# Expert passes cut in quarters of 32 rows, experts ordered on the chip by remainder, five weight buffers in both layers

## The chip, the cores and the metric

One Trainium2 chip, of which one core runs the kernel. The metric is the device time of one execution in microseconds (us). Three runs of the kernel before gave 2852.11, 2854.56 and 2857.07 us; their median is 2854.56 us.

## What is computed

A block of two layers over 512 latent tokens and 256 context tokens of 1024 numbers each, all in 32-bit floats. Each layer mixes the tokens (four groups of attention heads) and then sends each token through a mixture of experts. Only that second half is touched here:

```python
idx, wts = _route(h, w_r, b_r)          # sigmoid scores; 8 of 64 experts per token, from 4 of 8 groups
for each expert e:
    y = (silu(x @ wg[e]) * (x @ wu[e])) @ wd[e]      # x: the tokens that chose e; 1024 -> 256 -> 1024
    acc[tokens] += y * weight
f = acc + _swiglu(h, shared expert)
```

Layer 0 routes all 768 tokens (6144 choices of an expert), layer 1 only the 512 latent ones (4096 choices). How many tokens an expert gets is data. With the reference's own inputs the router gives experts 9 to 253 tokens. What matters below is the number of 32-row quarters that a count fills, modulo 4 ("the remainder"); experts 0 to 4 are kept apart, as the change treats them apart:

| | remainder 1 | remainder 2 | remainder 3 | remainder 0 | experts 0 to 4 |
|---|---|---|---|---|---|
| layer 0 | 11 experts | 9 | 21 | 18 | 102, 84, 77, 103, 130 tokens |
| layer 1 | 11 experts | 29 | 16 | 3 | 35, 57, 117, 36, 117 tokens |

Rounded up to halves of 64 rows, the counts fill 127 halves in layer 0 and 93 in layer 1.

## The kernel before

`build` runs, for each layer, the attention stages, then `route`, `experts` and `ffn_residual`. Each is a block in which every engine has its own program; semaphores order them.

`route` (lines 1206 to 1384) picks the experts on DVE, counts the tokens of each (PE, a product with ones), and turns the counts into a table in SBUF that the engines then read with register loads: for each pass the expert of its upper and of its lower 64 rows (`T_E0`, `T_E1`), a word that says which weight buffers it uses (`T_PASS`), the number of passes (`T_COUNT`), and for each expert the number of passes that must be over before its buffer may be loaded (`T_FREE`). An expert takes as many halves of 64 rows as it needs, at least one; the halves stand one behind another in the order of the experts, and two make a pass. DVE does this in a chain of small dependent operations (lines 1341 to 1382); PE helps with small products (1264 to 1281) and has the products of the shared expert (line 257) to do beside it.

`experts` (from 1387) runs a loop over passes, two to a turn, so that their number is rounded up to an even one. One pass i on the engines:

- PE: turns the gathered rows of pass i+1 (line 1555), forms the down products of pass i (1584), turns the hidden units (1562), makes the token list of pass i+3 (1550), and forms the gate and up products of pass i+1 (1575). Every matmul is made once for the upper and once for the lower 64 columns of the tile, `ps[h * HB:(h + 1) * HB, ...]` from buffer `w[h]`, also where both belong to one expert. Which buffers are meant is found by a tree of branches (`by_buffers`) over 2 x NB written-out variants, with NB the number of weight buffers.
- ACT and DVE: silu, the product with the up half, copies out of PSUM, the token list (`mark_slots`, `make_index`), the weight column, and the scaled result Y.
- POOL: one scatter of Y, which adds into `acc_dram` (line 1504), and one gather of the rows X of pass i+3 (1494). A scatter starts when the one before it has landed.
- SP: loads the weights, in the order of the experts, gate and up of expert e (2 MB) and down of e-1 (1 MB), each behind a wait until PE has done the last pass of the expert that held the buffer (`load_gate_up` 1448, `load_down` 1453).

There are five buffers in layer 0 and six in layer 1 (`BUFFERS = (5, 6)`). Buffers 3 and 4 are in use by the shared expert until the experts' stage has begun, so that their first experts come late.

Of the kernel before, what the change touches and what calls it, by code (L numbers as in the profile page):

```python
# [20 lines left out]
F16 = mybir.dt.float16  # L21
I32 = mybir.dt.int32
U32 = mybir.dt.uint32
ALU = mybir.AluOpType
# [3 lines left out]
P = 128  # L28
D = 1024
# [18 lines left out]
U = 2  # L48
STRETCH = 6
HB = P // 2  # L50
T_E0, T_E1, T_PASS, T_COUNT, T_FREE, T_TURNS, TAB_W = (
    1, TABN + 1, 2 * TABN, 4 * TABN, 4 * TABN + 1, 4 * TABN + 1 + E, 4 * TABN + 2 + E)
VAR = 256
AHEAD = 3
BUFFERS = (5, 6)
SHARED, TURNED, EARLY = 3, 4, 0
NTHR = NROW // HB
# [14 lines left out]
C_ID, C_COS, C_SIN, C_COSR, C_SINR, C_PREV, C_NEXT, C_BAND, C_P2, C_NEGP, C_NONE, C_NEGB, C_THR, C_ADD, C_SEL, C_W = (  # L72
    0, 128, 384, 640, 768, 896, 1024, 1152, 1216, 1218, 1219, 1220, 1348, 1360, 1361, 1363)

H_TRI, H_ONE, H_IOTA, H_TIN, H_TST, H_TSTHB, H_TOK, H_W = 0, 128, 256, 384, 448, 512, 576, 588
# [1130 lines left out]
def route(v, l, nt, gm, table, ex, shared):  # L1206
# [10 lines left out]
    s_sel, s_cnt, s_nb, s_slot, s_tab, s_tt = S("chosen"), S("counted"), S("blocks_counted"), S("slots"), S("table_columns"), S("table_turned")  # L1217
    counts = []
    with ExitStack() as scope:
# [9 lines left out]
        cc = sb("cc", [E, NTHR + 2])  # L1229
        nbb = sb("nbb", [E, P], F16)  # L1230
        o1 = sb("o1", [P, E])
        tb = sb("tb", [P, 12])
        fr = sb("fr", [1, E + 2])

        with nc.Block() as block:
# [20 lines left out]
            def _(pe):  # L1256
# [10 lines left out]

                s_nb.wait(pe, 1)
                pe.matmul(ps[:, 6, 0:E], nbb[:, :], csth[0:E, H_TIN:H_TIN + E], start=True, stop=True)
                for i in range(nt):  # L1270
                    out = ps[:, 7, i * E:(i + 1) * E]
                    pe.matmul(out, nbb[:, :], csth[0:E, H_TSTHB:H_TSTHB + E], start=True, stop=False)
# [3 lines left out]
                last.then_inc(s_slot.sem, 1)  # L1276
                shared.gate_up_products(pe, 2, 0)
                shared.gate_up_products(pe, 2, 1)
                s_tab.wait(pe, 1)
                for c in range(3):  # L1280
                    last = pe.matmul(ps[0:1, 6, c * P:(c + 1) * P], tb[:, c:c + 1], v.ident, start=True, stop=True)
# [9 lines left out]
            def _(dve):  # L1291
# [49 lines left out]
                step(dve.tensor_copy(cc[:, NTHR + 1:NTHR + 2], ps[0:E, 6, E:E + 1]))  # L1341
                step(dve.tensor_scalar(cc[:, 0:NTHR], v.cst[0:E, C_THR:C_THR + NTHR], cc[:, NTHR + 1:NTHR + 2], None, ALU.is_lt))
                step(dve.tensor_reduce(cc[:, NTHR:NTHR + 1], cc[:, 0:NTHR], AX, ALU.add))
                dve.tensor_scalar(nbb[:, :], csth[0:E, H_ONE:H_ONE + P], cc[:, NTHR:NTHR + 1], None, ALU.mult).then_inc(s_nb.sem, 1)
# [12 lines left out]
                for h in range(2):  # L1357
                    step(dve.tensor_scalar(o1[:, :], ps[:, 6, 0:E], v.cst[:, C_P2 + h:C_P2 + h + 1], None, ALU.is_le))
                    step(dve.tensor_reduce(tb[:, h:h + 1], o1[:, :], AX, ALU.add))
                step(dve.tensor_scalar(tb[:, 0:2], tb[:, 0:2], float(E - 1), None, ALU.min))  # L1360
                whole(tb[:, 5:6], tb[:, 0:1], 1.0 / NB, -0.5 + 0.5 / NB)
                step(dve.tensor_scalar(tb[:, 7:8], tb[:, 5:6], -float(NB), tb[:, 0:1], ALU.mult, ALU.add))
                step(dve.tensor_tensor(tb[:, 8:9], tb[:, 1:2], tb[:, 0:1], ALU.subtract))
                step(dve.tensor_scalar(tb[:, 2:3], tb[:, 7:8], 2.0, tb[:, 8:9], ALU.mult, ALU.add))
                step(dve.tensor_copy(tb[:, 9:10], ps[:, 6, E - 1:E]))
                whole(tb[:, 10:11], tb[:, 9:10], 0.5, 0.25)
                whole(tb[:, 11:12], tb[:, 9:10], 0.25, 0.375)
                step(dve.tensor_scalar(tb[:, 11:12], tb[:, 11:12], 16.0, None, ALU.mult))
                whole(fr[0:1, 0:E], ps[0:1, 6, 0:E], 0.5, 0.25)
                step(dve.memset(table[0:1, T_PASS:T_PASS + 2 * TABN], 0))  # L1370
                step(dve.memset(table[0:1, T_FREE:T_FREE + NB], 0))
                step(dve.tensor_copy(table[0:1, T_FREE + NB:T_FREE + E], fr[0:1, 0:E - NB]))
                step(dve.tensor_scalar(tb[:, 3:4], tb[:, 5:6], 16.0, 16.0, ALU.mult, ALU.add))
                dve.tensor_scalar(tb[:, 2:3], tb[:, 2:3], float(VAR), tb[:, 3:4], ALU.mult, ALU.add).then_inc(s_tab.sem, 1)
                shared.hidden_units(dve, 1)
                s_tt.wait(dve, 1)
                step(dve.tensor_copy(table[0:1, 0:2 * P], ps[0:1, 6, 0:2 * P]))
                by_pass = table[0:1, T_PASS:T_PASS + 2 * TABN].rearrange("a (p w) -> a w p", w=2)
                step(dve.tensor_copy(by_pass[:, 0, 1:TABN], ps[0:1, 6, 2 * P:3 * P - 1]))
                step(dve.tensor_copy(by_pass[:, 1, 0:TABN - 1], ps[0:1, 6, 2 * P + 1:3 * P]))  # L1380
                step(dve.tensor_copy(table[0:1, T_COUNT:T_COUNT + 1], tb[0:1, 10:11]))
                step(dve.tensor_copy(table[0:1, T_TURNS:T_TURNS + 1], tb[0:1, 11:12]))
    for s, k in ((s_step, counts[0]), (s_ex, 1), (s_wt, 1), (s_ws, 16), (s_clear, 3), (s_sel, 1), (s_cnt, 1), (s_nb, 1), (s_slot, 1), (s_tab, 1), (s_tt, 1)):
        s.stage_over(k)


def experts(v, l, nt, gm, table, ex, shared):
# [4 lines left out]
    pairs = ((nt * P * 8 + E * HB) // HB + 1) // 2  # L1392
# [16 lines left out]
    with ExitStack() as scope:  # L1409
# [9 lines left out]
        cur = sb("cur", [P, nt, 2])  # L1419
# [25 lines left out]
        with nc.Block() as block:  # L1445
            @block.sync
            def _(sp):
                def load_gate_up(w, e, free):
                    sp.wait_ge(gate_up, free + CREDIT)
                    sp.dma_start(wgu[w][:, :, :].rearrange("p k n -> p (k n)"),  # L1450
                                 v.t["exp_gu"][l][bass.ds(e, 1)].rearrange("a p n -> (a p) n")).then_inc(w_gu[w], 16)

                def load_down(w, e, free):
                    sp.wait_ge(down, free + CREDIT)
                    sp.dma_start(wd[w][:, :, :].rearrange("p k n -> p (k n)"),
                                 v.t["exp_d"][l][bass.ds(e, 1)].rearrange("a p n -> (a p) n")).then_inc(w_d[w], 16)
# [10 lines left out]
                sp.wait_ge(gate_up, free_after(NB) + CREDIT)  # L1467
                sp.dma_start(wgu[0][:, :, :].rearrange("p k n -> p (k n)"), v.t["exp_gu"][l, NB]).then_inc(w_gu[0], 16)
# [6 lines left out]
                for e in range(NB + 1 + rounds * NB, E):  # L1475
                    sp.wait_ge(gate_up, free_after(e) + CREDIT)
                    sp.dma_start(wgu[e % NB][:, :, :].rearrange("p k n -> p (k n)"), v.t["exp_gu"][l, e]).then_inc(w_gu[e % NB], 16)
# [519 lines left out]
```

## Time and profile before

| | |
|---|---|
| median of the runs | 2854.56 us |
| the profiled execution: its own time | 2857.52 us |
| its span in the trace | 2855.7 us |
| mean granted clock of TensorE | 0.961 |
| PE busy | 2586.1 us, 91% of the span |
| DVE, ACT, POOL busy | 38%, 20%, 14% |
| HBM read, written | 578.84 MB, 77.99 MB |

The layers stand one behind the other. The expert stage of layer 0 takes about 759 to 1554 us of the span, that of layer 1 about 2179 to 2825 us; `route` stands ahead of each. In the profile "L1575" is line 1575 of the kernel, "PEld" is TensorE's loading of the stationary operand, a 32-bit matmul appears as two records, and "issue" is idle time for which the profile shows no releaser.

### The profile page before, as it was taken

Reading aid. Unit: us, or ns where it says so; the run is one execution under the profiler, and the core shown is the slowest. Engines: PE = TensorE matmul, PEld = TensorE weight load, DVE = VectorE, ACT = ScalarE, POOL = GpSimd, SP = SyncE. Lnnn points to the kernel's source line nnn. Section 1 sums busy time; section 2 is a strip of 40 time slices with the busy share of each in tenths; the row PEclk is TensorE's granted clock in tenths of the full one; section 3 lists DMA queues with packets and bytes.
Section 4 is the critical chain, followed back from the end, with each engine's and each line's share of the span. In section 5 each row is a group of like instructions: output and inputs, shape, how many; then the busy total and the mean of one; then the engine's idle time right before and its main releaser. Section 6 shows DMA issues by size and latency. Waiting matters only on the chain. (4 is left out here: it accounts for less than half of the span.)

```text
span 2855.7 us, 44970 instructions
## 1 busy us (share of the span) xinstructions
PE 2586.1 (91%) x13801; PEld 1281.4 (45%) x13802; DVE 1084.5 (38%) x3199; ACT 585.4 (20%) x1378; POOL 386.9 (14%) x314
## 2 busy tenths in 40 slices
PE   6999989999899999999996588989997999899995
PEld 3566555645433333333332366666553333333331
DVE  3443351534333333333332743451543233233323
ACT  2222341411111111111111341331310111111111
POOL 0000001000022222222221200001000212112122
PEclk9999999999999999999998799999998999999998
DMA  7120203043688998999993402202346999998983
GB/s 273 58 93 30 113 21 143 4 181 128 228 281 310 344 327 281 325 325 323 335 371 98 172 1 93 89 16 116 115 178 251 351 394 398 396 392 306 382 319 112
DMA packets 104984, 619.35 MB, mean 217 GB/s; under 512 B 22832, under 2 KB 23088, under 8 KB 64688
## 3 DMA queue, kind: packets, MB, share of 16 engines
q1 hardware_dynamic: 69744, 525.06, 46.7%
q0 software_dynamic: 33696, 87.63, 12.7%
q10 hardware_dynamic: 1440, 5.24, 0.5%
q8 instruction: 69, 1.13, 0.2%
q14 instruction: 35, 0.29, 0.0%
HBM read 578.84 MB, written 77.99 MB: 230 GB/s over the span
## 5 line engine op out<-in xcount | busy, mean ns | idle before, releaser
L1575 PE MATMUL ps<-wgu,xT 128*64 128x512 f32 x2048 | 454.9, 597 | 3.1 <-issue 3.1
L1575 PE MATMUL ps<-wgu,SGx 128*64 128x512 f32 x1536 | 351.7, 610 | 22.5 <-DMA wgu<-in_exp_gu 18.3
L1504 POOL DMA_INDIRECT ffn_rows<-Y,six x114 | 182.5, 1601 | 1120.0 <-issue 651.1
L678 PE MATMUL ps<-w_in,wgu 128*128 128x512 f32 (+3 forms) x768 | 267.8, 509 | 15.0 <-PEq L435 3.8
L1575 PEld LDWEIGHTS ps<-wgu,xT 128*64 128x64 f32 x2048 | 141.8, 137 | 261.9 <-issue 260.7
L1584 PE MATMUL ps<-wd,hiddenT 128*64 128x512 f32 x1040 | 239.2, 602 | 5.6 <-issue 5.6
L1575 PEld LDWEIGHTS ps<-wgu,SGx 128*64 128x64 f32 x1536 | 110.6, 140 | 223.4 <-issue 217.0
L678 PEld LDWEIGHTS ps<-w_in,wgu 128*128 128x128 f32 x768 | 149.8, 198 | 124.9 <-issue 111.9
L1584 PE MATMUL ps<-wd,csil 128*64 128x512 f32 x784 | 180.6, 602 | 9.1 <-issue 8.5
L1758 DVE TENSOR_TENSOR hidden<-silu,ps 128x256 f32<-128x256 f32 x64 | 27.0, 421 | 375.8 <-ACT silu L1690 375.8
L1685 ACT ACTIVATE Y<-ps,wc 128x512 f32<-128x512 f32 x114 | 78.3, 687 | 421.6 <-PE ps L1584 421.6
L1752 DVE TENSOR_SCALAR Y<-ps,wc 128x512 f32<-128x512 f32 x114 | 85.6, 751 | 202.2 <-PE ps L1584 202.2
L1555 PEld LDWEIGHTS ps<-cst,X 128*128 128x128 f32 x912 | 99.2, 142 | 114.3 <-issue 70.0
L1555 PE MATMUL ps<-cst,X 128*128 128x128 f32 x912 | 126.4, 282 | 21.2 <-DMA X<-h_rows,gix 15.9
L1098 PE MATMUL ps<-w_in,oT 128*128 128x512 f32 x320 | 142.3, 605 | 0.0
L1758 DVE TENSOR_TENSOR small<-small,ps 128x256 f32<-128x256 f32 x48 | 20.2, 421 | 308.7 <-ACT small L1690 308.7
L1494 POOL DMA_INDIRECT X<-h_rows,gix x118 | 121.6, 1031 | 86.3 <-issue 35.0
L1584 PEld LDWEIGHTS ps<-wd,hiddenT 128*64 128x64 f32 x1040 | 69.4, 137 | 128.9 <-issue 128.9
L1690 ACT ACTIVATE silu<-ps 128x256 f32<-128x256 f32 x64 | 24.6, 384 | 428.6 <-PE ps L1575 428.6
L1718 DVE TENSOR_TENSOR mark<-csth,cur 128x384 f16<-128x384 f16 (+1 forms) x236 | 107.7, 498 | 4.1
L678 PE MATMUL ps<-w_in,wd 128*128 128x256 f32 (+5 forms) x384 | 102.6, 424 | 0.0
L1584 PEld LDWEIGHTS ps<-wd,csil 128*64 128x64 f32 x784 | 56.0, 137 | 100.5 <-issue 100.5
(496 smaller groups left out, 3077.2 us busy)
## 6 DMA issues: line engine op xcount, KB each, us to landing
wgu<-in_exp_gu SPq DMA_DIRECT2D x128, 2048.0 KB, 30.1
wd<-in_exp_d SPq DMA_DIRECT2D x128, 1024.0 KB, 9.3
wgu<-in_ada_w SPq DMA_DIRECT2D x40, 1024.0 KB, 4.9
ada_start<-in_ada_w SPq DMA_DIRECT2D x8, 1024.0 KB, 8.3
w_in<-in_w_in SPq DMA_DIRECT2D x4, 2048.0 KB, 10.1
w_in<-in_w_out SPq DMA_DIRECT2D x4, 2048.0 KB, 12.5
wgu<-ffn_rows SPq DMA_DIRECT2D x16, 512.0 KB, 8.8
w_in<-in_w_in SPq DMA_DIRECT2D x2, 3072.0 KB, 14.2
```

The costliest lines, as they stand in the source:

```text
L678: last = pe.matmul(pp[i % 2][:, at:at + c1 - c0], held.columns(k, i), wg[g % 2][:, k, c0:c1], start=(k == 0), stop=(k == KD - 1))
L1098: last = pe.matmul(ps[:, 2 * (i % 2) + n, :], oT[:, k, i * P:(i + 1) * P], w[n][:, k, 0:512], start=(k == 0), stop=(k == KD - 1))
L1494: pool.indirect_dma_start(out=X[j][:, :], out_offset=None, in_=v.h2_dram, in_offset=bass.IndirectOffsetOnAxis(ap=gix[j][:, 0:1], axis=0), ...
L1504: pool.indirect_dma_start(out=v.acc_dram, out_offset=bass.IndirectOffsetOnAxis(ap=six[j][:, 0:1], axis=0), in_=Y[j][:, :], in_offset=None, ...
L1555: last = pe.transpose(ps[:, 3 + k // 4, k % 4 * P:(k % 4 + 1) * P], X[j][:, k * P:(k + 1) * P], v.ident)
L1575: last = pe.matmul(ps[h * HB:(h + 1) * HB, 0, :], xT[:, k, h * HB:(h + 1) * HB], wgu[w[h]][:, k, :], start=(k == 0), stop=(k == KD - 1))
L1584: last = pe.matmul(ps[h * HB:(h + 1) * HB, 1 + c, :], G[:, f, h * HB:(h + 1) * HB], wd[w[h]][:, f, c * 512:(c + 1) * 512], start=(f == 0), ...
L1685: act.activation(Y[j][:, 0:512], ps[:, 1, :], ACT.Copy, scale=wc[j][:, 0:1]).then_inc(y_act, 1)
L1690: act.activation(SG[:, :], ps[:, 0, 0:FD], ACT.Silu).then_inc(silu, 1)
L1718: last = dve.tensor_tensor(mark[:, :, h * HB:(h + 1) * HB], iota, cur[:, :, h:h + 1].broadcast_to([P, nt, HB]), ALU.is_equal)
L1752: dve.tensor_scalar(Y[j][:, 512:D], ps[:, 2, :], wc[j][:, 0:1], None, ALU.mult).then_inc(y_dve, 1)
L1758: dve.tensor_tensor(HID[:, :], SG[:, :], ps[:, 0, FD:2 * FD], ALU.mult).then_inc(hidden, 1)
```

## The change

- Rows are counted in quarters of 32. A pass is one expert's (kind 0, matmuls over all 128 columns), two experts' 64/64 (kind 1), or two experts' 96/32 (kind 2, three matmuls, of 64, 32 and 32 columns).
- The experts are done in another order: 0 to 4 as before in halves; then those of remainder 2 (and of remainder 1 without a partner, rounded up); then pairs of one expert of remainder 3 and one of remainder 1; then those that fill whole passes (remainder 0, and 3 without a partner, rounded up). A key for each expert, a comparison of all keys and a few products give the order, in `route`.
- SP reads the expert to load from the table (`T_ORDER`), one register load more for each of the two loads of an expert. DVE reads three experts a pass in place of two, and one flag (`T_SPLIT`) that picks the row offsets of the scatter; it marks slots and fills the weight column in three pieces.
- `by_buffers` has 3 x NB variants. NB is 5 in both layers.

The diff, cut to its core:

```diff
-BUFFERS = (5, 6)
+BUFFERS = (5, 5)
+SEGMENTS = ((0, 64), (64, 32), (96, 32))
+KINDS = 3
...
+                step(dve.tensor_scalar(cc[:, :], cst[0:EP, C_THR:C_THR + 2 * NTHR], count, None, ALU.is_lt))
+                step(dve.tensor_reduce(cls[:, 1:3], cc[:, :].rearrange("p (a n) -> p a n", a=2), AX, ALU.add))
+                step(dve.scalar_tensor_tensor(out=r, in0=f, scalar=-4.0, in1=b, op0=ALU.mult, op1=ALU.add))
+                dve.tensor_scalar(kk[:, :], cst[0:EP, C_CLASS:C_CLASS + 5], r, None, ALU.is_equal).then_inc(s_rows.sem, 1)
...
+                s_products.wait(dve, 1)
+                step(dve.tensor_copy(cls[:, 16:21], ps[0:EP, 4, 0:5]))
+                step(dve.tensor_tensor(below, cls[:, 16:18], cls[:, 18:20], ALU.is_lt))
...
+                dve.tensor_scalar(less[:, 0:E], ps[0:EP, 5, 0:E], key, float(QB), ALU.is_gt, ALU.mult).then_inc(s_nb.sem, 1)
...
                 def load_gate_up(w, e, free):
+                    weights = placed(e)
                     sp.wait_ge(gate_up, free + CREDIT)
...
+                def placed(e):
+                    return sp.value_load(table[0:1, bass.ds(e + T_ORDER, 1)], min_val=0, max_val=E - 1)
...
+                def row_groups(w):
+
+                    if w[2] == w[0]:
+                        return [(slice(0, P), w[0])]
+                    if w[1] == w[2]:
+                        return [(slice(0, HB), w[0]), (slice(HB, P), w[2])]
+                    return [(slice(at, at + n), w[m]) for m, (at, n) in enumerate(SEGMENTS)]
+
                 def gate_up_products(w, count):
                     wait_weights(w_gu, w, count)
                     for k in range(KD):
-                        for h in range(2):
-                            last = pe.matmul(ps[h * HB:(h + 1) * HB, 0, :], xT[:, k, h * HB:(h + 1) * HB], wgu[w[h]][:, k, :],
-                                             start=(k == 0), stop=(k == KD - 1))
+                        for group, b in row_groups(w):
+                            last = pe.matmul(ps[group, 0, :], xT[:, k, group], wgu[b][:, k, :], start=(k == 0), stop=(k == KD - 1))
...
                     if n == 1:
-                        products((a // 2, (a // 2 + a % 2) % NB), count)
+                        own, kind = a // KINDS, a % KINDS
+                        other = (own + 1) % NB
+                        products(((own, own, own), (own, other, other), (own, own, other))[kind], count)
...
-                    for h in range(2):
+                    for h in range(NS):
                         dve.tensor_scalar(cur[:, :, h], gm[:, :, bass.ds(es[h], 1)].rearrange("p t a -> p (t a)"),
...
-                    e1, e3 = entries(i + 1), entries(i + AHEAD)
+                    e1, e3, second = entries(i + 1), entries(i + AHEAD), split(i - 1)
```

## Rows read from the trace of the kernel before

**Rows 1.** The page: span, and GB/s in 40 equal slices
```profile
span 2855.7 us, 44970 instructions
GB/s 273 58 93 30 113 21 143 4 181 128 228 281 310 344 327 281 325 325 323 335 371 98 172 1 93 89 16 116 115 178 251 351 394 398 396 392 306 382 319 112
```

**Rows 2.** Busy time by stretch of the expert stages, first line the columns
```profile
core 0: us, PE busy (x) PEld busy (x) DVE busy (x) ACT busy (x) POOL busy (x), PEclk, DMA share, GB/s
917.00:1537.00 620.00, 618.08 (x3264) 234.45 (x3264) 223.10 (x714) 92.30 (x204) 134.17 (x102) 1.00 0.92 314
...
2179.00:2242.00 63.00, 54.20 (x251) 21.30 (x250) 15.54 (x51) 7.29 (x16) 7.91 (x6) 0.89 0.74 260
...
2286.00:2450.00 164.00, 156.09 (x798) 60.18 (x800) 53.08 (x182) 23.17 (x51) 33.73 (x26) 1.00 1.02 395
2450.00:2550.00 100.00, 89.48 (x438) 33.87 (x434) 28.78 (x98) 12.68 (x28) 18.78 (x15) 0.93 1.01 400
```

**Rows 3.** PE in time, a pass of layer 0 (start, us, work)
```profile
1148.39 1.09 PE L1555 MATMUL ps<-cst,X 128*128 128x128 f32 x8
...
1153.49 7.09 PE L1575 MATMUL ps<-wgu,xT 128*64 128x512 f32 x32
1160.51 1.10 PE L1555 MATMUL ps<-cst,X 128*128 128x128 f32 x8
```

**Rows 4.** Line 1575: ns min/median/max, first and last start, by layer
```profile
L1575 PE MATMUL ps<-wgu,xT x2048: 592/592/1115, 758.8 to 1537.0; 128*64 128x512 f32 x187
...
L1575 PE MATMUL ps<-wgu,SGx x1536: 590/592/1116, 2179.1 to 2811.8; 128*64 128x512 f32 x192
```

**Rows 5.** DMA issues by line: count, KB each, us to landing
```profile
wgu<-in_exp_gu SPq DMA_DIRECT2D x128, 2048.0 KB, 30.1
```

**Rows 6.** PE in time, layer 1, idle before in brackets
```profile
2195.43 10.13 PE L1575 MATMUL ps<-wgu,SGx 128*64 128x512 f32 x32 [4.23 <-issue]
...
2222.34 1.97 PE L1555 MATMUL ps<-cst,X 128*128 128x128 f32 x8 [4.25 <-issue]
...
2229.88 1.51 PE L1575 MATMUL ps<-wgu,SGx 128*64 128x512 f32 x6
...
2464.10 9.93 PE L1575 MATMUL ps<-wgu,SGx 128*64 128x512 f32 x32 [6.88 <-DMA wgu<-in_exp_gu]
```

**Rows 7.** PE with other tile widths, a group and a timeline piece
```profile
L1098 PE MATMUL ps<-w_in,oT 128*128 128x512 f32 x320 | 142.3, 605 | 0.0
...
29.48 1.93 PE L348 MATMUL ps<-ada_start,csil 128*32 128x256 f32 x16
```

**Rows 8.** DVE in order of time, route of layer 0
```profile
708.74 0.14 DVE L1341 COPY cc<-ps 64x1 f32<-64x1 f32 x1
...
709.37 0.25 DVE L1344 TENSOR_SCALAR nbb<-csth,cc 64x128 f16<-64x128 f16 x1
...
714.19 0.15 DVE L1353 TENSOR_SCALAR tb<-tb 128x1 f32<-128x1 f32 x1
714.38 0.15 DVE L1354 TENSOR_SCALAR tb<-tb 128x1 f32<-128x1 f32 x1
...
720.92 0.14 DVE L1382 CAST table<-tb 1x1 int32<-1x1 f32 x1
```

**Rows 9.** DVE in time, start of the experts, layer 0
```profile
725.56 0.37 DVE L1713 TENSOR_SCALAR cur<-gm,cst 128x6 f32 x2 [3.50 <-issue]
...
733.50 0.60 DVE L1713 TENSOR_SCALAR cur<-gm,cst 128x6 f32 x2 [1.14 <-issue]
```

**Rows 10.** DVE and PE inside one pass of layer 0
```profile
905.10 0.42 DVE L1758 TENSOR_TENSOR hidden<-silu,ps 128x256 f32<-128x256 f32 x1 [5.74 <-ACT silu L1690]
...
906.70 1.03 DVE L1718 TENSOR_TENSOR mark<-csth,cur 128x384 f16<-128x384 f16 x2
...
909.45 0.29 PE L1550 MATMUL ps<-csth,mark 128*128 128x2 f16 x6
```

**Rows 11.** The page: the queue that carries instructions
```profile
q8 instruction: 69, 1.13, 0.2%
```

More of the change, by code:

```diff
@@ new lines, in _ @@
+                count, b, f, r, k12, key, paired, odd, turn2 = (cls[:, n:n + 1] for n in range(9))
+                below, place, own = cls[:, 10:12], cls[:, 12:14], cls[:, 14:16]
+                step(dve.memset(cls[E:EP, 0:1], 0.0))
+                step(dve.tensor_copy(cls[0:E, 0:1], ps[0:E, 6, E:E + 1]))
+                step(dve.tensor_scalar(cc[:, :], cst[0:EP, C_THR:C_THR + 2 * NTHR], count, None, ALU.is_lt))
+                step(dve.tensor_reduce(cls[:, 1:3], cc[:, :].rearrange("p (a n) -> p a n", a=2), AX, ALU.add))
@@ new lines, in _ @@
+                step(dve.tensor_tensor(below, below, kk[:, 0:2], ALU.mult))
+                step(dve.scalar_tensor_tensor(out=place, in0=cls[:, 16:18], scalar=2.0, in1=own, op0=ALU.mult, op1=ALU.add))
+                step(dve.tensor_tensor(place, place, below, ALU.mult))
+                step(dve.tensor_reduce(paired, place, AX, ALU.add))
+                step(dve.tensor_tensor(key, key, paired, ALU.add))
+                dve.tensor_scalar(keyd[0:E, :], cst[0:E, C_ID:C_ID + E], cls[0:E, 5:6], None, ALU.mult).then_inc(s_rows.sem, 1)
@@ new lines, in _, with whole @@
+                step(dve.tensor_reduce(paired, below, AX, ALU.add))
+                step(dve.tensor_tensor(b, b, paired, ALU.subtract))
+                step(dve.tensor_tensor(odd, cls[:, 19:20], cls[:, 18:19], ALU.subtract))
+                step(dve.scalar_tensor_tensor(out=odd, in0=odd, scalar=0.0, in1=cls[:, 20:21], op0=ALU.max, op1=ALU.add))
+                def whole(out, src, by, shift):
+                    step(dve.tensor_scalar(out, src, by, shift, ALU.mult, ALU.add))
+                    step(dve.tensor_scalar(out, out, 12582912.0, None, ALU.add))
+                    step(dve.tensor_scalar(out, out, -12582912.0, None, ALU.add))
@@ new lines, in _ @@
+                dve.scalar_tensor_tensor(out=tb[:, NS + 1:NS + 2], in0=tb[:, 12:13], scalar=float(VAR), in1=tb[:, 14:15],
+                                         op0=ALU.mult, op1=ALU.add).then_inc(s_tab.sem, 1)
+                step(dve.tensor_copy(tb[:, 16:17], ps[:, 6, E:EP]))
+                whole(tb[:, 17:18], tb[:, 16:17], 1.0 / P, 0.375)
+                whole(tb[:, 18:19], tb[:, 16:17], 0.5 / P, 0.4375)
+                step(dve.tensor_scalar(tb[:, 18:19], tb[:, 18:19], 16.0, None, ALU.mult))
@@ L1382, in _ @@
-                step(dve.tensor_copy(table[0:1, T_TURNS:T_TURNS + 1], tb[0:1, 11:12]))
-    for s, k in ((s_step, counts[0]), (s_ex, 1), (s_wt, 1), (s_ws, 16), (s_clear, 3), (s_sel, 1), (s_cnt, 1), (s_nb, 1), (s_slot, 1), (s_tab, 1), (s_tt, 1)):
+                step(dve.tensor_copy(by_pass[:, 0, 1:TABN], ps[0:1, 5, P:2 * P - 1]))
+                step(dve.tensor_copy(by_pass[:, 1, 0:TABN - 1], ps[0:1, 5, P + 1:2 * P]))
+                step(dve.tensor_copy(table[0:1, T_COUNT:T_COUNT + 1], tb[0:1, 17:18]))
@@ new lines, in _ @@
+                step(dve.tensor_copy(table[0:1, T_TURNS:T_TURNS + 1], tb[0:1, 18:19]))
+                step(dve.tensor_copy(table[0:1, T_ORDER:T_ORDER + E], ps[0:1, 5, E:2 * E]))
+                whole(fr[0:1, 0:E], ps[0:1, 5, 0:E], 1.0 / P, 0.375)
+                step(dve.tensor_copy(table[0:1, T_FREE + NB:T_FREE + E], fr[0:1, 1:E - NB + 1]))
+    for s, k in ((s_step, counts[0]), (s_ex, 1), (s_wt, 1), (s_ws, 16), (s_clear, 3), (s_sel, 1), (s_cnt, 1), (s_nb, 1), (s_slot, 1), (s_tab, 1), (s_tt, 1),
+                 (s_products, 2), (s_rows, 3)):
@@ L1582, in down_products @@
                         for c in range(2):
-                            for h in range(2):
-                                last = pe.matmul(ps[h * HB:(h + 1) * HB, 1 + c, :], G[:, f, h * HB:(h + 1) * HB],
-                                                 wd[w[h]][:, f, c * 512:(c + 1) * 512], start=(f == 0), stop=(f == 1))
+                            for group, b in row_groups(w):
+                                last = pe.matmul(ps[group, 1 + c, :], G[:, f, group], wd[b][:, f, c * 512:(c + 1) * 512], start=(f == 0), stop=(f == 1))
                     last.then_inc(down, 1)
```

231 lines of the change are left out of this document (138 added, 93 removed).

## Prediction

> **What bounds the kernel now.** I read the page first: the span of 2855.7 us and the traffic in its 40 slices, which shows two long loaded stretches, one per layer [rows 1]. They are the expert stages. Their busy times by stretch show two different limits [rows 2]. In layer 0, between 917 and 1537 us, PE is busy for 618.08 of 620 us at full clock, while DMA moves 314 GB/s at a share of 0.92: PE is the bound. In layer 1, between 2286 and 2450 us, DMA stands at a share of 1.02 and 395 GB/s (400 in the stretch behind it) and PE has gaps: DMA is the bound. I take 397 GB/s as what DMA can give.
>
> A pass of layer 0 lasts 1160.51 - 1148.39 = 12.12 us from turn to turn, 7.09 of it gate and up products [rows 3]. Line 1575 is there 2048 and 1536 times; a pass makes 16 matmuls in 32 records, so that is 64 and 48 passes, which agrees with 127 and 93 halves, paired and rounded up to an even number [rows 4]. From the first to the last gate-up start layer 0 takes 1537.0 - 758.8 = 778 us, where 63 periods and a matmul series need about 770; layer 1 takes 2811.8 - 2179.1 = 633 us where 47 periods and a series need 574. So layer 0 loses nearly nothing to waits, layer 1 some 59 us.
>
> **Part 1, fewer passes: the count.** Experts of remainder 1 and 3 in one pass save a half each pair: min(11, 21) = 11 pairs in layer 0 and min(11, 16) = 11 in layer 1. Summed in quarters by the diff's rules, layer 0 fills 232 and layer 1 164, that is 58 passes in place of 64, and 41, run as 42, in place of 48. At 12.12 and 12.07 us (layer 1 without waits) PE's work falls by 73 and 72 us. The bytes do not fall: every expert is still 3.15 MB (2048 KB of gate and up [rows 5] and half as much of down), and a gather and a scatter skip empty rows (4352 and 4096 bytes for each real row, 8448 together).
>
> **Part 2, layer 0.** What is left is 58 periods of PE work, if weights keep up. On average they do: 59 loaded experts and 6144 rows are 185.6 + 51.9 = 237.5 MB, 598 us at 397 GB/s, against 703 us. But the new order bunches the demand. By the counts, passes 0 to 5 use positions 0 to 5, passes 6 to 11 two new experts each (positions 6 to 17), passes 11 to 28 about one each (an expert of remainder 1 here mostly has a whole pass of its own too), the rest one or fewer. Five buffers look ahead no further than five experts. When pass 6 starts, positions up to 8 are in; 9 to 17 must land by the start of pass 11: 9 x 3.15 + about 505 rows x 8448 = 32.6 MB, 82 us, where PE has 5 x 12.12 = 61. That is a wait of about 22 us, and with the clock that falls in it (below) 25. Layer 0: -73 + 25 = -48. Bounds: -73 if the wait is hidden, -35 if a gather or a pair costs as much again.
>
> **Part 3, layer 1.** Here the order does the opposite of smoothing. Fixed experts and remainder 2 come first, then pairs: except one, each of passes 4 to 29 brings two new experts (positions up to 55), and passes 30 to 41 bring eight between them. The two-expert passes need 6.29 MB and some 99 rows, 7.1 MB, which is 18.0 us against 12.07 of PE. DMA sets their pace; then it is idle while PE does the last twelve at its own. The sum: up to pass 3 the order is about as before, and its gate-up starts at 2229.88, 51 us after the first (the stretch has 4 us idles behind which no DMA stands [rows 2, 6]). Then positions 8 to 55 are loaded, 151.0 MB, with about 2570 rows, 21.7 MB: 172.7 MB, 435 us. The last two-expert pass starts at 51 + 435 = 486, and twelve periods and a series behind it end at 486 + 145 + 7 = 638 us, against 633 now. The sixth buffer goes as well: one expert more, 7.9 us at 397 GB/s, that could have come early; it is in the sum, as five buffers hold positions 3 to 7 at pass 3. With a few us of late gathers I take layer 1 at +8. Bounds: -15 (DMA gets ahead as far as position 10 by pass 3: two experts, 16 us, and no late gather) and +30 (380 GB/s in place of 397 is +20, and more gathers late).
>
> **Part 4, matmul forms.** A whole pass has 8 matmuls of 128 columns in place of 16 of 64. Line 1098 is such a group: 142.3 us for 320 records, 0.445 each, 16 of them 7.1 us, as now [rows 7]: no gain. 96/32 passes have 24, of 64, 32 and 32 columns. Mixed widths are not in the trace; the nearest rows are four of 32 columns side by side: 16 records of 256 columns in 1.93 us, a rate that only tiles running together give [rows 7]. I take them at nothing, between 0 and a full series more per pair pass (+7 us; 11 passes in layer 0, those in layer 1 partly under DMA).
>
> **Part 5, route.** It is on the path, with a chain on DVE and PE waiting for its end. A small dependent step costs 0.19 us [rows 8]. Ahead of the slot products there are 4 steps from 708.74 to 709.62; the new text has 33, mostly small ones, 6.7 us: +5.9, and +0.4 for more products. Behind them four steps more and wider ones, +1.0; behind the turned table five steps and a copy twice as wide, +1.1. The shared expert's products that covered this are not longer, so it is all in the open: +8.4 in layer 0 and +7.7 in layer 1, where one PE wait is covered. At the start of the experts DVE's register loads show as idle: 1.14 us for two, 3.50 for four with what else is there [rows 9]. Three loads more in layer 0 are 1.7 us, with three small operations 2.2; in layer 1 only those ahead of the first gather count, 1.2. Sum +19.5; bounds +14 (steps overlap) and +26. DMA isn't helped by the delay: its next loads wait for passes.
>
> **Part 6, hidden in the loop.** DVE does seven loads a pass in place of four and three small operations more: about 1.7 + 0.5 us. It waits 5.74 us for silu ahead of the hidden product, and marks end 1.7 us before PE lists them [rows 10]. Only 0.3 us of the addition lies in that second stretch. Cost nothing; if the cover were gone, 2 us a pass. SP's loads of the order stand ahead of its waits, with transfers queued. Nothing.
>
> **The sum.** Layer 0 -48, layer 1 +8, route +19.5: -20.5, so 2857.5 - 20.5 = 2837 for an execution like the profiled one. That one is 3.0 us above the median of 2854.56, which gives 2834.
>
> **Rivals.**
>
> 1. *DMA keeps ahead.* If layer 0's wait is hidden or layer 1 starts further ahead (-73 and -15, route +19): -69, 2786; in part, about 2805. For: the layers' DMA has slack at their starts, 260 GB/s in the first 63 us of layer 1 [rows 2]. Against: the buffers, not DMA, set that slack.
> 2. *PE's clock falls in the 18 us passes* (ends slower). PE would idle for 6 us of each. After idles of 4.25 and 6.88 us the turn took 1.97 in place of 1.09 us, and a gate-up series 9.93 in place of 7.09 [rows 6]: 2.4 GHz had become 1.2. That is a factor of up to 1.8 on 12.07 us, where 18.0 / 12.07 = 1.49 is free. If one stretch a pass is slow, 15 us, DMA still decides. If most of the pass is, some 20 us, twenty-five passes cost +50: 2884. Mixed widths that run one after another would give the same sign, 11 x 7 = +77 in layer 0 at most. The Trainium skill (TensorE: Matmul & The Clock Gate, HAM oscillation) describes a kernel that falls to the low clock in every DMA wait; by it each two-expert pass pays. The trace agrees in the idles of these rows, but the series behind them ends at 2.4 GHz again: 9.93 us is not twice 7.09.
> 3. *Even.* DMA gives 380 to 385 GB/s under the new mixture and layer 0 waits longer: about +15 on the sum, 2850.
> 4. *PE's code does not stay on the engine.* The variants' matmuls grow from 12 x 24 to 15 x 24 per loop in layer 1 (10 x 24 in layer 0). Now 69 packets of instructions for the whole span [rows 11] say that the loop is not fetched again. If it were, an idle like the 4.23 us at the loop's first rounds [rows 6] would come in each of 100 passes: +420, 3250. The Trainium skill (Runtime: NRT & Kernel Launch, Instruction fetch mechanics) gives PE room for 2048 instructions; at four a 32-bit matmul the new loop is by my estimate some 1650, so it would fit.
> 5. *It doesn't do what it says:* passes not fewer, only route's +19.5: 2874.
>
> **Chances.** Forecast (2818 to 2848) 0.45; rival 1 0.17; rival 3 0.14; rival 2 0.15; rival 4 0.06; rival 5 0.03. 0.2% is 5.7 us, about what a measurement can tell from no change. Faster 0.62, same 0.14, slower 0.24. The range leaves out rival 4, the far ends of 1 and 2: 2800 to 2878.
>
> **What would show it.** Line 1575 in 58 and 42 passes; periods of about 18 us in layer 1 between passes 6 and 29, DMA at 1.0 there and far below in the last 140 us; waits for wd or wgu between passes 9 and 12 of layer 0; route's chain 8 us longer. Wrong would make it: periods of 20 us at a granted clock of 0.5 to 0.8, instruction packets all through the loops, or gate-up series over 7.1 us in the pair passes of layer 0.

## The result: 13% slower, and where the time went

The changed kernel takes 3223.97 us (median of 4 runs, 3220.15 to 3233.79) beside 2855.6 us for the kernel before in the same session: a ratio of 1.1297, 95% interval 1.127 to 1.1325. I had forecast 2834 us, and my range ended at 2878. It was wrong by 390 us and in its sign.

The page of the changed kernel, against [rows 1, 11]: the span, PE's line of the first part, and the queue that carries instructions.

```profile
span 3222.5 us, 43453 instructions
...
PE 2768.0 (86%) x12245; PEld 1331.5 (41%) x12246; DVE 1081.5 (34%) x3421; ACT 563.2 (17%) x1330; POOL 354.7 (11%) x290
...
q8 instruction: 170, 2.79, 0.4%
```

The span is 366.8 us longer than the 2855.7 of before, and there are 170 instruction packets in place of 69: 2.79 MB, so 16 KB each, which is 256 of the compiled program's instructions of 64 bytes. The passes did fall to 58 and 42, as counted: silu's and the hidden product's lines stand there 58 and 42 times.

Where the engine was, in time. A piece of two 96/32 passes of layer 1, the down series of one and the gate-up series of the next (start, length, line, shape of the first instruction, count, idle before in brackets):

```profile
2804.17 1.09 PE L1638 MATMUL ps<-cst,X 128*128 128x128 f32 x8
2805.19 8.01 PE L1674 MATMUL ps<-wd,csil 128*64 128x512 f32 x24
2813.13 0.44 PE L1645 MATMUL ps<-cst,small 128*128 128x128 f32 x2
2813.40 0.24 PE L1633 MATMUL ps<-csth,mark 128*128 128x2 f16 x4
2813.58 15.95 PE L1666 MATMUL ps<-wgu,SGx 128*64 128x512 f32 x48
```

The gate-up series of a 96/32 pass takes 15.95 us and its down series 8.01, where those of before take 7.09 [rows 3] and 3.65:

```profile
1149.41 3.65 PE L1584 MATMUL ps<-wd,hiddenT 128*64 128x512 f32 x16
```

Nothing waits in this piece: the tiles themselves take the time. There are 11 such passes in each layer.

The same engine in layer 0, in a stretch of whole passes, none of them mixed:

```profile
1429.78 1.97 PE L1638 MATMUL ps<-cst,X 128*128 128x128 f32 x8 [10.99 <-issue]
1433.59 5.50 PE L1674 MATMUL ps<-wd,hiddenT 128*128 128x512 f32 x8 [1.84 <-issue]
1438.92 0.38 PE L1645 MATMUL ps<-cst,hidden 128*128 128x128 f32 x2
1439.14 0.29 PE L1633 MATMUL ps<-csth,mark 128*128 128x2 f16 x6
1446.70 9.21 PE L1666 MATMUL ps<-wgu,xT 128*128 128x512 f32 x16 [7.26 <-issue]
```

Here the series are short where the clock holds, but PE stands idle for 10.99, 1.84 and 7.26 us with no releaser, and after the long idles the work runs at 1.2 in place of 2.4 GHz (1.97 us for a turn that takes 1.09 elsewhere). The waits of PE over layer 0's loop (total, times, longest), and then the instruction queue in each loop, 760 to 1778 us and 2415 to 3177 us:

```profile
PE ps L1638 <- issue: 76.6, 22, 12.1
PE ps L1674 <- issue: 38.8, 21, 12.4
PE ps L1666 <- issue: 28.8, 17, 7.7
```

```profile
q8 instruction: 102, 1.67, 0.7%
...
q8 instruction: 7, 0.11, 0.1%
```

Layer 0's loop brought 102 packets of 16 KB, layer 1's only 7; before it was 5 and 8. So there are two causes to separate: tiles of different widths (both layers), and PE's code being fetched again (layer 0 only). Stretches of layer 1 show a third, smaller thing (columns as in [rows 2]):

```profile
2505.00:2740.00 235.00, 175.92 (x779) 66.18 (x776) 58.03 (x221) 23.55 (x52) 34.06 (x26) 0.87 1.00 390
...
2740.00:3043.00 303.00, 303.00 (x1024) 68.91 (x1024) 55.88 (x213) 22.65 (x50) 31.44 (x24) 0.99 0.75 280
```

Two-expert passes at 64/64 are bound by DMA (share 1.00, 390 GB/s, PE busy 176 of 235 us), as I had said for all of them. The 96/32 passes behind them are not: PE is busy for 303.00 of 303 us. The doubled series have used up the cover that DMA would have given.

### The profile page after: what moved, and what is told of

Same layout as the page of the kernel before. It is cut to its first block and busy times, and to the rows that moved or that the text cites. A ratio compares the mean times of both kernels' runs of the same rounds, so it can differ in the third digit from the quotient of the medians.

```text
span 3222.5 us, 43453 instructions
## 1 busy us (share of the span) xinstructions
PE 2768.0 (86%) x12245; PEld 1331.5 (41%) x12246; DVE 1081.5 (34%) x3421; ACT 563.2 (17%) x1330; POOL 354.7 (11%) x290
## 3 DMA queue, kind: packets, MB, share of 16 engines
q8 instruction: 170, 2.79, 0.4%
## 5 line engine op out<-in xcount | busy, mean ns | idle before, releaser
L1666 PE MATMUL ps<-wgu,xT 128*128 128x512 f32 (+2 forms) x1360 | 517.3, 608 | 28.9 <-issue 28.8
L1666 PE MATMUL ps<-wgu,SGx 128*64 128x512 f32 (+2 forms) x1296 | 423.6, 646 | 72.5 <-DMA wgu<-in_exp_gu 59.1
L1587 POOL DMA_INDIRECT ffn_rows<-Y,six x102 | 163.0, 1598 | 1504.4 <-issue 1438.2
L1674 PE MATMUL ps<-wd,hiddenT 128*128 128x512 f32 (+2 forms) x688 | 284.7, 651 | 38.9 <-issue 38.8
L1666 PEld LDWEIGHTS ps<-wgu,xT 128*128 128x128 f32 (+2 forms) x1360 | 167.8, 157 | 332.5 <-issue 332.0
L1666 PEld LDWEIGHTS ps<-wgu,SGx 128*64 128x64 f32 (+2 forms) x1296 | 118.4, 147 | 343.9 <-issue 330.6
L1674 PE MATMUL ps<-wd,csil 128*64 128x512 f32 (+2 forms) x664 | 206.1, 604 | 9.7 <-issue 9.7
L1674 PEld LDWEIGHTS ps<-wd,hiddenT 128*128 128x128 f32 (+2 forms) x688 | 88.2, 167 | 195.9 <-issue 195.9
L1674 PEld LDWEIGHTS ps<-wd,csil 128*64 128x64 f32 (+2 forms) x664 | 54.9, 139 | 129.9 <-issue 129.9
L1809 DVE TENSOR_TENSOR mark<-csth,cur 128x192 f16<-128x192 f16 (+3 forms) x318 | 104.1, 383 | 3.6
```

The lines of the kernel that those rows point to most:

```text
L1587: pool.indirect_dma_start(out=v.acc_dram, out_offset=bass.IndirectOffsetOnAxis(ap=six[j][:, 0:1], axis=0), in_=Y[j][:, :], in_offset=None, ...
L1666: last = pe.matmul(ps[group, 0, :], xT[:, k, group], wgu[b][:, k, :], start=(k == 0), stop=(k == KD - 1))
L1674: last = pe.matmul(ps[group, 1 + c, :], G[:, f, group], wd[b][:, f, c * 512:(c + 1) * 512], start=(f == 0), stop=(f == 1))
L1809: last = dve.tensor_tensor(mark[:, :, at:at + n], iota, cur[:, :, h:h + 1].broadcast_to([P, nt, n]), ALU.is_equal)
```

## The experiments

e4, e5, e12 and e16 start from the kernel before, e9 to e11 from it with the new scheme added for layer 0, the rest from the changed kernel. All have the run-time test of e1. Places and lengths of loops are counted in the compiled program. Where a layer's time is given, it runs from the start of its first down series to the end of its last. Before: 786.8 us in layer 0, 636.1 in layer 1, 633.5 between them.

**e1: the base.**

```
- table[...], engines=[PE], min_val=0, max_val=KINDS * NB * VAR, skip_runtime_bounds_check_because="..."
+ table[...], engines=[PE], min_val=0, max_val=KINDS * NB * VAR
```

> The changed kernel, with the one difference that the words TensorE loads for a pass are bounded by a test at run time (a few more instructions per pass on TensorE's sequencer). It is the base of the other runs. Both theories: within 10 us of the 3224 us of the changed kernel. Theory W (mixed widths): the gate-up series of a 96/32 pass takes 15.9 us and the down series 8.0 us against 7.1 and 3.6, 22 such passes. Theory C (TensorE's code): about 170 instruction packets of TensorE's queue, nearly all the extra ones in layer 0's loop, which costs it some 130 us of idle time.

Measured: 3085.97 us, ratio 1.081 (1.0791 to 1.0828); 76 instruction packets, 9 in layer 0's loop and 7 in layer 1's. Each loop on PE has four instructions more and begins 4 (layer 0) or 16 (layer 1) instructions later, and the kernel is 138 us faster. The widths are as before (15.9 and 8.0 us), the fetches are gone. Both theories had expected 3224 us. The miss was the first hint that not only the amount of code matters, but also where it lies.

**e2: four tiles of 32 columns.**

```
- return [(slice(at, at + n), w[m]) for m, (at, n) in enumerate(SEGMENTS)]
+ return [(slice(at, at + QB), w[m]) for at, m in ((0, 0), (QB, 0), (2 * QB, 1), (3 * QB, 2))]
```

> A 96/32 pass is computed as four tiles of 32 columns (own, own, own, other) in place of one of 64 and two of 32. Theory W (a 64-column tile and 32-column tiles do not run beside each other, tiles of one width do): the gate-up series falls from 15.9 to about 7.1 us and the down series from 8.0 to 3.6; 11 x 13.2 = 145 us less in layer 0, and in layer 1 up to the 112 us by which it lies above the forecast, the rest being under the transfers: about 3224 - 145 - 112 = 2967 us if the code is fetched as now. Rival to W (each product costs some 331 ns whatever its tile, so that 48 take 15.9 us): 64 products take 21.2 us, +5.3 and +2.6 a pass, about 3224 + 22 x 7.9 = 3400 us. Theory C: the loop grows from 1664 to 1904 instructions on TensorE, so layer 0 is fetched at least as much as now, and layer 1's loop is now fetched too: 2967 plus another 130 or so, 3100 us.

Measured: 3776.24 us, ratio 1.3211. Both halves of the expectation are there, at other sizes. The shortest gate-up series of 64 products takes 7.1 us and the shortest down series 3.6, so four equal tiles do run side by side. But 234 and 272 packets came in the two loops, far more than I had priced.

```profile
q8 instruction: 565, 9.26, 1.2%
```

**e3: the changed kernel as I had forecast it.**

```
- if w[1] == w[2]:
+ if w[2] != w[0]:
```

> A 96/32 pass is computed as two tiles of 64 columns, the second with the other expert's weights: rows 64 to 95 are multiplied with the weights of the wrong expert, the rest, the waits, transfers, passes and their order are those of the changed kernel. The loop on TensorE shrinks from 1664 to 1424 instructions. This is the changed kernel as my forecast took it. Theory W alone (the widths cost, the fetches come from the order in which variants are used): 2967 us, with some 170 instruction packets. Theories W and C together: no fetches in the loops (about 75 packets) and 3224 - 145 - 132 - 112 = 2835 us. Neither: 3224.

Measured: 2862.16 us, ratio 1.0026 (1.0014 to 1.0038), 71 packets. It is the "both" case but for 27 us. By stage, against the kernel before: 7.4 us later into layer 0's loop, 44.9 us less in it, 7.9 us more between the layers, 34.4 us more in layer 1. That sums to +4.8, and the spans differ by 4.6. So even with both surprises taken away the change would have brought nothing.

**e4: code that no pass takes, in the kernel before.**

```
- BUFFERS = (5, 6)
+ BUFFERS = (5, 5)
+ KINDS = 3
...                                     # the word of a pass and the three trees: KINDS for 2
- products((a // 2, (a // 2 + a % 2) % NB), count)
+ own = a // KINDS
+ products((own, (own + (0, 1, 1)[a % KINDS]) % NB), count)
```

> The kernel before with five weight buffers in both layers, and with a third variant per buffer in TensorE's loop that no pass takes (24 products each, so that its loops have the same 1664 instructions in nearly the same places as the changed kernel's). Theory C by length (the loop of layer 0 no longer stays on the engine when it is that long): some 100 instruction packets more than the 69 of before and 100 to 140 us more, all in layer 0, about 2980 us. Theory C by use (what matters is which variants are taken, so code that is skipped costs nothing): 2856 us plus what five buffers for six cost in layer 1, 0 to 15 us, and 70 to 75 packets.

Measured: 3285.0 us, ratio 1.1514 (1.1487 to 1.1541), 279 packets. "By use" is refuted: with instructions that are never executed the kernel takes 415 us more than e5 below, which has all but them. But "by length" had the wrong layer: layer 0's loop stayed (9 packets), layer 1's brought 212. PE's waits over layer 1's loop:

```profile
PE ps L1556 <- issue: 181.9, 24, 13.4
PE ps L1576 <- issue: 136.6, 20, 15.2
PE ps L1585 <- issue: 63.6, 26, 7.8
```

These are 382 us, at the turn, the gate-up and the down series alike, wherever a branch leads into code that is not there.

**e5: five buffers in both layers, old order.**

```
- BUFFERS = (5, 6)
+ BUFFERS = (5, 5)
```

> The kernel before with five weight buffers in both layers, nothing else. In e3 layer 1, from its first down series to its last, took 670.5 us where the kernel before takes 636.1, a loss of 34 us that is neither widths nor code. Theory B (the sixth buffer): layer 1 goes from 636 to about 670 us here too, 2890 us in all. Rival O (the order, all experts of two halves first): layer 1 stays at 636 to 640 us, 2856 us. Code: loops of 5 and 6 blocks of 256 instructions, no fetches in the loops, 68 to 71 packets.

Measured: 2869.78 us, ratio 1.0046 (1.0029 to 1.0062). Layer 1 takes 643.1 us, 7 more than before. So most of e3's 34 us isn't the sixth buffer by itself.

**e6 and e7: the same code, half a block and one block later.** Ahead of layer 0's loop on PE:

```
+ if l == 0:
+     with pe.If(turns16 < 1):          # never so
+         for n in range(250):          # e7: 504
+             pe.wait_ge(x_act, 1)
```

> The kernel of e1 with a branch never taken ahead of layer 0's loop on TensorE, whose instructions move everything behind it by 129 instructions. Nothing that is executed changes but one compare. Counted in the compiled program in blocks of 256 instructions (the 16 KB of one instruction packet), both loops are 6.5 blocks long; in e1 each lies in seven blocks (31.10 to 37.60, 64.48 to 70.96), here each reaches into an eighth (31.60 to 38.10, 64.98 to 71.46). Theory S (a loop stays on the engine while it touches seven blocks, and is fetched anew when it touches eight): both loops are fetched in every few passes, 200 to 500 packets in all; by the changed kernel's layer 0 (96 extra packets, 138 us) and e4's layer 1 (some 205 packets, 430 us) that is 3086 + 280 to 860, about 3500 us. Rival L (the length or the variants matter, or e1's run-time test did it in another way): 3086 us and 76 packets.

> The same branch with twice the instructions, so that everything behind it lies exactly 256 instructions later than in e1: 32.10 to 38.60 and 65.48 to 71.96, seven blocks each. Theory S: 3086 us as e1, 77 packets. If more code in the program or the branch itself costs: above e6's loss, or 3086 plus half of it.

Measured: e6 3084.83 us (ratio 1.0798), 9 and 7 packets; e7 3126.74 us (1.0946), 26 and 7. Both are misses of theory S. The placement that should have been worst changed nothing, and the one that should have been neutral cost 41 us. Seven blocks touched against eight is not the rule. Yet e7 executes what e6 executes, so place does matter.

**e8: e3 with six buffers in layer 1.**

```
- BUFFERS = (5, 5); FIXED = 5
+ BUFFERS = (5, 6); FIXED = 6
```

> e3 (pair passes as two tiles of 64 columns, rows 64 to 95 with the wrong expert's weights) with six weight buffers in layer 1, the first six experts in fixed places; the route's small tiles of layer 1 lie in free gather buffers to make room. Theory B (the sixth buffer is what layer 1 lacks): layer 1 from 670 to about 640 us, 2832 us in all, which is the forecast of the change. Rival O (the order makes the transfers the bound whatever the buffers): 665 to 671 us, 2860 us.

Measured: 2851.24 us, ratio 0.9987 (0.9971 to 1.0002). Layer 1 takes 653.4 us: the sixth buffer gives back 17 of the 34 us. The other 17 stay with six buffers and six fewer passes. I put them down to the order, though no run changes the order alone. PE's waits for gate and up weights in layer 1, first in e3, then in e8; before it was 18.3 us, 5 times:

```profile
PE ps L1666 <- DMA wgu<-in_exp_gu: 99.6, 22, 8.3
```

```profile
PE ps L1668 <- DMA wgu<-in_exp_gu: 85.6, 19, 8.1
```

**e9, e10, e11: the new scheme in layer 0 alone, three ways to compute a 96/32 pass.** Layer 1 keeps everything of the kernel before; layer 0 has four buffers, so that its loop stays clear of fetches in all three.

```
+ BUFFERS = (4, 6); Q_VAR = 512         # layer 0 only: route and experts as changed
e9:  for k: for at, m in ((0, 0), (32, 0), (64, 1), (96, 2)): a tile of 32 columns
e10: for k: tiles of 64, 32 and 32 columns, as in the change
e11: for k: the tile of 64;  then for k: the two tiles of 32
```

> The new scheme in layer 0 alone, with four weight buffers there (so that its loop on TensorE is 1566 instructions, 6.1 packets) and the 96/32 passes as four tiles of 32 columns; layer 1 keeps the route, order, passes and six buffers of the kernel before. Theory W: gate-up series 7.1 and down series 3.6 us in every kind of pass; theory C: no fetches in either loop, about 71 packets. From e3, which has the same passes in layer 0: 7.4 us later into the loop, 45 us less in it; a fourth buffer for five costs between 0 and 20 us; layer 1 as before. 2856 + 7 - 45 + 0 to 20 = 2818 to 2838, I take 2825 us. Rival (four tiles side by side are slower than two, or the four buffers eat the gain): 2850 us or more.

> e9 with the 96/32 passes as in the changed kernel, a tile of 64 columns and two of 32 for each step of the sum. Nothing else differs, and the loop is shorter than e9's. Theory W: 11 such passes at 15.9 and 8.0 us for 7.1 and 3.6: 11 x 13.2 = 145 us above e9, about 2970 us, no fetches. Rival (e2's four tiles were no test, because of the fetches): no more than 20 us from e9.

> e10 with the products of a 96/32 pass in another order: first all steps of the 64-column tile, then all steps of the two 32-column tiles. Theory W1 (tiles of different widths never run beside each other, and the three tiles take as long as two whole series): gate-up 7.1 + 7.1 = 14.2 us, down 7.1 us, 11 x (1.7 + 0.9) = 29 us under e10. Theory W2 (each change of width costs, and is the whole of it): one change for 15, gate-up near 7.1 + 8.8 / 15 = 7.7 us plus what the tiles lose by not overlapping; anything near 8 us, and the time within 20 us of e9, speaks for it. Theory W3 (a product costs 331 ns whatever the order): 15.9 us and e10's time.

Measured: e9 2831.28 us, ratio 0.9911 (0.9894 to 0.9927); e10 2956.24 us, 1.0344 (1.0326 to 1.0361); e11 2928.33 us, 1.0256 (1.0238 to 1.0273). They have 69, 70 and 70 packets. e10 lies 125 us above e9 where 145 were expected: PE is busy 143.5 us longer in layer 0 (840.7 for 697.2), and some of its idles are gone. e11 lies 28 us below e10, for 29. One gate-up series of a 96/32 pass in each, in this order:

```profile
1014.08 7.07 PE L2276 MATMUL ps<-wgu,xT 128*32 128x512 f32 x64
```

```profile
1059.91 15.95 PE L2276 MATMUL ps<-wgu,xT 128*64 128x512 f32 x48
```

```profile
1049.36 14.07 PE L2281 MATMUL ps<-wgu,xT 128*64 128x512 f32 x48
```

Sixty-four products of 32 columns take 7.07 us; forty-eight products of mixed widths take 15.95. Grouped by width they take 14.07, which is 7.07 twice: the 64-column tile as long as a whole series, then the two others together. Interleaved they had the chance to overlap and took longer still. So a tile of 64 and tiles of 32 did not run beside each other here, and each change of width costs a little on top: (15.95 - 14.07) us for 15 changes in place of one, 0.13 us each. That is W1; W2 and W3 are refuted. e9 is 0.9% faster than the kernel before, a small gain, but its interval is clear of 1: layer 0 takes 748.5 us for 786.8, its loop begins 8.0 us later, and layer 1 is the old one.

**e12, e13, e14: place.** The never-taken branch of e6 again: before e4's loop with 250 waits, before e1's with 122 and with 378.

> e4 (the kernel before with five buffers and a variant that no pass takes) with everything from layer 0's loop on moved 129 instructions later on TensorE by a branch never taken. What is executed is e4's. Theory P (where a loop of some 1690 instructions lies decides whether it is fetched again): layer 1's loop, fetched 212 times in e4, lies as far into a block as e6's, which stayed: no fetches in either loop, about 75 packets and e5's 2865 us, 420 us less than e4. Rival (the dead variant itself sets it off): 3285 us and about 280 packets.

> The kernel of e1 moved a quarter of a block later (layer 0's loop 31.27 to 37.89, layer 1's 64.65 to 71.26). Theory P says only that the time is 3085 us where both loops stay and more where one does not, with the packets counted in that loop; of ten loops of this length seven stayed so far. A third outcome, more time without more packets, would speak against the packets as the measure of it.

> The same by three quarters of a block (31.77 to 38.39, 65.15 to 71.76). As for e13: 3085 us with about 76 packets if both loops stay; 41 us more came with 16 packets in e7, 138 us more with 93 in the changed kernel, 430 us with 203 in e4, so each further packet in a loop costs 1.5 to 2.6 us of time.

Measured: e12 2885.07 us (1.0086), 400 us less than e4 by moving the same code 129 instructions; e13 3398.69 us (1.1884); e14 3508.49 us (1.2268), each of the last two the median of two runs. In e13 it is layer 1 that is fetched, in e14 layer 0. The same executed work, in three places, takes 3085, 3399 and 3508 us.

**The model, and e15 and e16.** Thirteen kernels gave 26 loops. A count of packets was worked out for each from the compiled program and the known order of variants. The model keeps eight blocks of 256 instructions and drops the one unused for longest. It fetches the next block once execution is some way into one (56 instructions in layer 0, 40 in layer 1). The base of the blocks is 4 instructions less than the program's count in layer 0 and 32 more in layer 1. Those four numbers were fitted. Put shortly: a loop stays while the blocks it touches, with the one fetched ahead behind its end, are eight at most, and is fetched anew when they are nine. By this a loop of up to 1576 instructions would stay wherever it lies; no run tried one between 1566 and 1688. Then two places that it had not seen:

> The kernel of e1 with everything from layer 0's loop on moved 32 instructions later (layer 0's loop 31.14 to 37.77, layer 1's 64.52 to 71.13). A model was fitted to the packets counted in the 26 loops of the runs so far: eight blocks of 256 instructions are kept, the one not used for longest goes, and the next block is fetched once execution is about a fifth of a block into one. It says 8 packets in layer 0's loop and 210 in layer 1's. In time, by e13 (206 packets, 314 us above e1): 3400 us. Rival (place decides, but not by this): anything else, such as both loops staying, 3085 us.

> The kernel of e4 (the old work, with a variant never taken) moved 208 instructions later (layer 0's loop 31.86 to 38.48, layer 1's 65.27 to 71.88). In e4 layer 0's loop stayed and layer 1's was fetched 212 times. The fitted model says that they change places: 331 packets in layer 0's loop and 8 in layer 1's. In time, by e12 (2885 us where nothing is fetched) and e4 and e14 (1.8 to 2.0 us for each further packet): 2885 + 323 x 1.9 = 3500 us, between 3380 and 3560. Rival: layer 1 still the one that is fetched, or both.

Measured: e15 3375.8 us (1.1822) and e16 3547.17 us (1.2422), of two runs each. The instruction queue of e15 in layer 1's loop, of e16 in layer 0's and in layer 1's:

```profile
q8 instruction: 193, 3.16, 1.4%
```

```profile
q8 instruction: 329, 5.39, 1.8%
...
q8 instruction: 7, 0.11, 0.1%
```

The model said 210, 331 and 8. The loops that it said would stay did, and the two layers of e4's code changed places. Two simpler models don't fit. Without the fetch ahead a loop of 6.6 blocks never touches more than eight, and none would be fetched again. With the block dropped that was fetched first, the best fit gives 206 packets for the 329 of e16's layer 0 and 139 for the 212 of e4's layer 1. The loops that matter, with the loops of e15 and e16 among them (those left out have 5 to 9 packets and 6 to 8 by the model). Lengths and places are of the whole loop with the branches that close it; the expectations of e1 to e7 go by an earlier count (1664 for 1696, places up to 0.1 block off):

| kernel, layer | loop, in blocks | instructions | packets | model |
|---|---|---|---|---|
| before, 0 | 31.04 to 35.53 | 1152 | 5 | 6 |
| before, 1 | 61.55 to 66.86 | 1362 | 8 | 7 |
| e3, 0 | 31.02 to 36.70 | 1456 | 8 | 7 |
| changed, 0 | 31.00 to 37.61 | 1692 | 102 | 41 |
| changed, 1 | 64.34 to 70.93 | 1688 | 7 | 8 |
| e1, 0 | 31.02 to 37.64 | 1696 | 9 | 8 |
| e7, 0 | 32.02 to 38.64 | 1696 | 26 | 8 |
| e6, 0 | 31.52 to 38.14 | 1696 | 9 | 8 |
| e14, 0 | 31.77 to 38.39 | 1696 | 235 | 241 |
| e16, 0 (seen after) | 31.86 to 38.48 | 1696 | 329 | 331 |
| e4, 1 | 64.46 to 71.07 | 1692 | 212 | 218 |
| e15, 1 (seen after) | 64.52 to 71.13 | 1692 | 193 | 210 |
| e13, 1 | 64.65 to 71.26 | 1692 | 206 | 223 |
| e12, 1 | 64.96 to 71.57 | 1692 | 7 | 8 |
| e8, 1 | 63.15 to 69.89 | 1726 | 7 | 8 |
| e2, 0 | 31.02 to 38.58 | 1936 | 234 | 231 |
| e2, 1 | 65.65 to 73.19 | 1932 | 272 | 287 |

The changed kernel's layer 0 and e7's lie on the model's edge. With the base one to three instructions lower it gives 41 to some 180 for the first, and 8 or 41 for e7, so there it says only that the place is bad. What stays open: why the base differs between the layers, and why e1 and e7, exactly 256 instructions apart, do not behave alike.

## Why the prediction was wrong, point by point

From the kernel before to the changed one by spans: before to e3 +4.6, e3 to e1 +221.2 (mixed widths in 22 passes), e1 to the changed kernel +141.0 (fetches in layer 0). That is 366.8 us, the whole of it.

1. **Part 1 was right.** The passes and their own price held: in e9 whole passes have series of 7.1 and 3.6 us.
2. **Part 4 is the step that failed first.** "Mixed widths are not in the trace; ... I take them at nothing, between 0 and a full series more per pair pass (+7 us...)". The measured cost is 8.9 us in the gate-up series and 4.4 in the down series: 13.2 a pass, nearly twice my upper bound. The row that I leaned on [rows 7] has tiles of one width. It shows that equal tiles run together, and says nothing of unequal ones. I had also put no price at all on the down products. e3 to e1 is 130.0 us in layer 0, where PE is the bound and 11 x 13.2 is 145, and 91.4 in layer 1, where DMA hid more of it. The same part's "no gain" for whole passes was a little off too (point 7). The same mechanism stood as one sentence in rival 2, at +77 at most, without a chance of its own.
3. **Rival 4 was real, at another size.** I had 0.06 for it, and the size all or nothing: +420 for every one of 100 passes. It came in one layer and in part, 141 us. The Trainium skill (Runtime: NRT & Kernel Launch, Instruction fetch mechanics) gives PE room for 2048 instructions, and the eight blocks of 256 that fit the runs are as many. My estimate of 1650 for the loop was near (1692), and the conclusion that it would fit was not right: with its place and the block fetched ahead it needs nine blocks. Loops up to 1566 stayed in every run here; those from 1688 to 1726 stayed or not by their place, and those of 1932 and 1936 never did. The same section says that a taken branch to a target outside a window of two pages stalls the engine until that page has been fetched. On the stall the trace agrees, with 382 us of such idles in e4. On the two pages it doesn't: in the kernel before, layer 1's loop lies over six blocks and brought 8 packets in 48 passes.
4. **Part 2 was right.** Layer 0 at -48: e3 has -44.9. The wait is there as well, at the ninth to twelfth gate-up series: 18.7 us in 4 times, for weights, where I had 22.
5. **Part 3 had the right mechanism and too small a size.** I forecast 18.0 us for a two-expert pass; e3 has 18.7 (from the gate-up starting at 2238.0 to that at 2594.1, 19 passes), at a DMA share of 1.00 and 385 GB/s where I had taken 397. The last two-expert pass starts 504 us after the first gate-up, not 486. Layer 1 came out at +34.4 for +8, just outside my bound of +30. With six buffers it is +17.3 (e8): what came with the new order costs more than the six saved passes bring.
6. **Part 5 was near.** The route's chain on DVE grew from 12.3 us (708.74 to 721.06) to 22.3 (707.16 to 729.45). The steps ahead of the slot products take 6.6 us (707.16 to 713.76), as forecast. Of the two waits for PE's products, the first was there before (2.21 us, for 2.23); the second grew from 0.32 to 2.15 us, which I had not counted. But less of it is seen outside: e3 enters its loops 7.4 and 7.9 us later, 15.3 in all for my 19.5.
7. **Part 6** costs nothing that can be seen: in e3 the last 28 periods of layer 0 are 11.6 to 13.2 us, 12.0 on average and half of them at 11.6 to 11.8, against 12.12 before [rows 3]. Where nothing waits, a whole pass of 128-column tiles is 0.5 us shorter than one of two 64-column tiles, a gain that part 4 had put at nothing; short idles take most of it back.
8. **Rival 2, the clock.** In layer 1's two-expert stretch the granted clock is 0.87 and DMA decides all the same. It is no part of the loss there.

My sum without part 4 and rival 4 was -20.5; e3 measured +4.6. So the forecast would have been 25 us off, inside its range. The 362 us beyond that come from a form of instruction and a length of code for which the trace of before had no row. I gave the first a narrow price, and the second a chance of 0.06, because nothing spoke for it. Both stood among the signs that would show me wrong. Both were the points where I had no measurement, and that is where the range should have been wide.

## What to carry to other kernels

Split a pass over several experts in tiles of one width: four of 32 columns took 7.07 us, as one of 128 does, while one of 64 and two of 32 took 15.95. Before adding variants to a loop on PE, count its instructions in the compiled program: at 1696 the same work took 3085 to 3508 us here by its place alone, loops up to 1566 stayed in every run, and nothing between was run. Four buffers in e9 kept the loop at 1566. A cost for which the trace has no row is where the range has to be wide, and when stages have different bounds, put the new scheme only where the stage is bound by what it saves, as e9 does for 0.9%.

## What the runs showed of the hardware that I had not expected

- Tiles of 64 and of 32 columns did not overlap: 15.95 us interleaved, 14.07 grouped, 7.07 where all are 32 wide. A change of width adds about 0.13 us.
- PE's code behaved like eight blocks of 256 instructions with the next one fetched ahead. A loop of 6.6 blocks stayed or thrashed by where it lay: 7 to 9 packets, or 193 to 329, with two places on the edge (26 and 102). The loss was 1.5 to 2.4 us for each further packet (e16 662 us for 320, e13 313 us for 197, e7 41 us for 17, the changed kernel 138 us for 93).
- Instructions that are never executed cost time if the loop around them is long and lies badly: e4 takes 400 us more than e12, the same code 129 instructions later. Where the loop stays on the engine, such code and its branches cost 11 to 15 us (e12 against e5, by ratios and by times).
